# Down projections of two MLPs by Strassen's scheme, with the block sums on GpSimd

## What is computed

```
def _sqrelu_mlp(h, w1, w2):
    u = jax.nn.relu(h @ w1)
    return (u * u) @ w2
...
        h = h + _sqrelu_mlp(_rmsnorm(h, mlp_norm_g[i]), mlp_w1[i], mlp_w2[i])
```

## Time and profile before

| | us |
|---|---|
| median of 3 runs | 2151.53 |
| lowest and highest | 2151.14, 2152.66 |
| the profiled execution | 2150.84 |
| its span, first to last instruction | 2149.2 |
| PE busy in the span | 2111.7 |
| DVE, ACT, POOL busy | 1237.6, 847.6, 294.5 |

### The profile page before, as it was taken

How to read it: one execution, slowest core, us unless ns; L and a number is a source line. 1 busy time by engine, 2 the same in 40 slices (tenths; PEclk the granted TensorE clock), 3 DMA queues, 4 the chain that set the end, 5 groups by cost and what they waited for, 6 DMA issues and landing times.

```text
span 2149.2 us, 27349 instructions
## 1 busy us (share of the span) xinstructions
PE 2111.7 (98%) x9798; PEld 1749.3 (81%) x9798; DVE 1237.6 (58%) x1837; ACT 847.6 (39%) x1363; POOL 294.5 (14%) x330
## 2 busy tenths in 40 slices
PE   8999999999999999999999999999999999999998
PEld 6888888788888888777888888877888888888887
DVE  6464554663454553887645445557765456656674
ACT  4433343432222344776322222447662234433342
POOL 3223132300000011443100000302310010000001
PEclk9999999999999999999999999999999999999999
DMA  5232323233333232222233232321223322333332
GB/s 191 74 98 74 98 64 98 70 115 111 117 101 117 89 103 89 89 74 73 93 99 98 88 103 93 104 84 55 74 78 104 90 96 89 112 104 117 98 97 70
DMA packets 58530, 203.53 MB, mean 95 GB/s; under 512 B 6937, under 2 KB 9129, under 8 KB 58448
## 3 DMA queue, kind: packets, MB, share of 16 engines
q1 hardware_dynamic: 54304, 189.82, 28.1%
q0 software_dynamic: 3712, 11.95, 1.7%
q10 hardware_dynamic: 432, 0.66, 0.1%
HBM read 200.27 MB, written 6.06 MB: 96 GB/s over the span
## 4 chain that ended last, share of the span: by engine, by line
PE 90%; DVE 4%; ACT 4%; issue 1%; POOL 0%; DMA 0%; DVEq 0%; ACTq 0%; POOLq 0%
PE bank L520 29%; PE bank L521 28%; PE bank L522 28%; PE bank L755 1%; DVE w_lo L1535 1%; ACT arena L1245 1%; ACT arena_r L1264 1%; ACT w_hi L1055 1%; PE bank L770 1%; PE bank L768 1%; PE bank L734 0%; ACT arena_r L1258 0%; DVE arena L1789 0%; DVE h L1585 0%; POOL arena L2274 0%
## 5 line engine op out<-in xcount | busy, mean ns | idle before, releaser
L1535 DVE TENSOR_TENSOR w_lo<-raw,w_hi 128x1024 fp32r<-128x1024 f32 x354 | 462.4, 1308 | 272.4 <-ACT w_hi L1055 272.1
L520 PE MATMUL bank<-x_hi,w_hi 128*128 128x512 f32 x1552 | 613.7, 395 | 1.4 <-issue 0.7
L522 PE MATMUL bank<-x_hi,w_lo 128*128 128x512 f32 x1552 | 604.5, 390 | 0.0
L521 PE MATMUL bank<-x_lo,w_hi 128*128 128x512 f32 x1552 | 604.1, 389 | 0.0
L1055 ACT ACTIVATE w_hi<-raw 128x1024 fp32r<-128x1024 f32 x354 | 371.2, 1052 | 386.2 <-PE bank L522 385.1
L520 PE MATMUL bank<-arena_r,w_hi 128*128 128x512 f32 (+1 forms) x1040 | 400.1, 385 | 6.0 <-DVE h L1585 2.7
L522 PE MATMUL bank<-arena_r,w_lo 128*128 128x512 f32 (+1 forms) x1040 | 398.0, 383 | 0.0
L521 PE MATMUL bank<-arena_r,w_hi 128*128 128x512 f32 (+1 forms) x1040 | 397.9, 383 | 0.0
L520 PEld LDWEIGHTS bank<-x_hi,w_hi 128*128 128x128 f32 x1552 | 291.5, 188 | 64.2 <-issue 4.2
L521 PEld LDWEIGHTS bank<-x_lo,w_hi 128*128 128x128 f32 x1552 | 291.6, 188 | 61.7 <-issue 3.1
L522 PEld LDWEIGHTS bank<-x_hi,w_lo 128*128 128x128 f32 x1552 | 291.3, 188 | 61.3
(11 more groups left out here) (230 smaller groups left out, 1989.4 us busy)
## 6 DMA issues: line engine op xcount, KB each, us to landing
raw<-in_stream SPq DMA_DIRECT2D x354, 512.0 KB, 3.5
arena<-in_rel_pad POOLq DMA_DIRECT2D x16, 256.0 KB, 3.2
bias_strips<-bias_strip_once POOLq DMA_DIRECT2D x12, 320.0 KB, 4.2
out_t<-h SPq DMA_DIRECT2D x8, 256.0 KB, 2.2
h<-in_x_t SPq DMA_DIRECT2D x6, 256.0 KB, 8.4
arena<-in_c_decay POOLq DMA_DIRECT2D x4, 256.0 KB, 2.9
arena<-bias_strips POOLq DMA_DIRECT2D x4, 256.0 KB, 4.3
arena<-bias_strips POOLq DMA_DIRECT2D x8, 128.0 KB, 2.4
```

Of the source, the lines that this page charges most:

```text
L520: pe.matmul(dst, lh, rh, start=start, stop=False, **kw)
L521: pe.matmul(dst, lh, rl, start=False, stop=False, **kw)
L522: return pe.matmul(dst, ll, rh, start=False, stop=stop, **kw)
L1535: dve.tensor_tensor(w_lo[:, s, :], raw[:, s, :], f32(w_hi[:, s, :]), ALU.subtract).then_inc(lo_ready, 1)
```

## The change

A down stage multiplies the 1024 x 1024 block of w2 by a 1024 x 512 activation matrix. It is now cut into pairs: the positions into two halves of 256 (`QUARTER`), the hidden tiles into even and odd ones, the output tiles into pairs n = 0 to 3. For each pair of output tiles that is a 2 x 2 by 2 x 2 block product, A (weights) times B (activations), made with seven products in place of eight:

- weight blocks of 128 x 512: A11, A12, A21, A22 are the four halves of two units (the hidden tiles are reordered on the host so that a unit's halves are the even and the odd ones); S1 = A21 + A22, S2 = S1 - A11, S3 = A11 - A21, S4 = A12 - S2;
- activation blocks of 128 x 256 for each of four k: B11, B21, B22, and T1 to T4, sums of these.

The eight sums are made by GpSimd in fp32 (`combos`, `block_sums`). Each block is then rounded by ACT (`combo_his`, `block_his`) and its low part made by DVE (`combo_los`, `block_los`), for seven activation blocks and seven weight blocks. `w_hi` and `w_lo` hold eight block slots now. A product is 4 k-steps of three matmuls of 256 columns. Products with the same place in the output accumulate in banks 4 to 7; after each one or two products DVE adds the bank to a half of a tile of h (`add`, L1943), 31 additions a stage, counted in `quarter_read`, and PE waits for that count before it goes on in the bank. The arithmetic saves products that are partial sums of others by adding a bank more than once.

The core of the diff:

```diff
-                    proj(us, first=[(u_lo, Lin(base, 8, i))])
-                    for _ in range(7):
-                        proj(us)
+                    down_seven(Lin(g, 1, i))
                     for _ in range(8):
                         proj()
...
+            def product(slot, b, bank, fresh, ready, read=None, combos=None):
+                (wh, wl), (of, count) = block_at(slot), ready
+                wait(pe, of, count)
+                if read is not None:
+                    wait(pe, quarter_read, read)
+                for kk in range(4):
+                    if combos is not None:
+                        wait(pe, combo_lo, combos + 5 * kk)
+                    a = kk * P
+                    m = mm3(banks[bank][:, 0:QUARTER], (wh[:, a:a + P], wl[:, a:a + P]), tuple(combo(kk, b)),
+                            fresh and kk == 0, kk == 3, False)
+                m.then_inc(products_done, 1)
+                at.pe = at.pe + 1
+
+            def down_seven(g):
+                u, made, rd = at.u, g * 20, g * 31
+                product(0, B11, 4, True, (block_lo, made + nth_a11(0)), combos=made + 1)
+                product(2, T1, 6, True, (block_lo, made + nth_s1(0)), combos=made + 2)
+                product(3, B21, 7, True, (block_lo, made + nth_a12(0)), combos=made + 3)
+                product(5, T2, 4, False, (block_lo, made + nth_s2(0)), rd + 1, combos=made + 4)
+                product(6, B22, 6, False, (lo_ready, u + 1), rd + 2)
+                for n in range(1, 4):
+                    x, x_old, seen = 4 + n % 2, 5 - n % 2, rd + (7 * n - 2)
+                    product(0, B11, x, True, (block_lo, made + nth_a11(n)), seen - 2 if n > 1 else None)
+                    if n == 1:
+                        wait(pe, combo_lo, made + 20)
+                    product(1, T3, x_old, False, (block_lo, made + nth_s3(n - 1)), seen - 1)
+                    product(2, T1, 6, True, (block_lo, made + nth_s1(n)), seen)
+                    product(3, B21, 7, True, (block_lo, made + nth_a12(n)))
+                    product(4, T4, x_old, False, (lo_ready, u + 2 * n), seen + 2)
+                    product(5, T2, x, False, (block_lo, made + nth_s2(n)))
+                    product(6, B22, 6, False, (lo_ready, u + (2 * n + 1)), seen + 3)
+                product(7, T3, 4, True, (block_lo, made + nth_s3(3)), rd + 24)
+                product(4, T4, 7, True, (lo_ready, u + 8))
...
+                def add(bank, j, half, done, behind=None):
+                    wait(dve, products_done, p + done)
+                    if behind is not None:
+                        wait(dve, quarter_read, rd + behind)
+                    part = h[:, j, half * QUARTER:(half + 1) * QUARTER]
+                    dve.tensor_tensor(part, banks[bank][:, 0:QUARTER], part, ALU.add).then_inc(quarter_read, 1)
...
+            def combos(g, kk):
...
+                pool.tensor_tensor(t1, even[:, QUARTER:S], even[:, 0:QUARTER], ALU.subtract).then_inc(combo_sum, 1)
...
+                pool.tensor_tensor(t2, odd[:, QUARTER:S], t1, ALU.subtract).then_inc(combo_sum, 1)
...
+                pool.tensor_tensor(t3, odd[:, QUARTER:S], even[:, QUARTER:S], ALU.subtract).then_inc(combo_sum, 1)
...
+                pool.tensor_tensor(t4, odd[:, 0:QUARTER], t2, ALU.subtract).then_inc(combo_sum, 1)
...
+            def block_sums(g, n, u):
...
+                pool.tensor_tensor(s1f, weights(u, 1, 0), weights(u, 1, 1), ALU.add).then_inc(block_sum, 1)
...
+                pool.tensor_tensor(s2f, s1f, weights(u, 0, 0), ALU.subtract).then_inc(block_sum, 1)
+                pool.tensor_tensor(weights(u, 1, 0), weights(u, 0, 0), weights(u, 1, 0), ALU.subtract)\
+                    .then_inc(block_sum, 1)
...
+                pool.tensor_tensor(s4f, weights(u, 0, 1), s2f, ALU.subtract).then_inc(block_sum, 1)
```

297 lines of the change are left out of this document (249 added, 48 removed).

## The result

The changed kernel takes **2199.42 us** (median of 4 runs, 2197.32 to 2200.59) against 2151.9 for the kernel before in the same comparison. The ratio is 1.022, 95% interval 1.0202 to 1.0237: slower by 2.2%. The profiled execution took 2199.88 us; its span is 2198.2, which is 49.0 more than the 2149.2 of the earlier trace rows.

What follows compares the result with a forecast made beforehand. PE was taken to bound the kernel by matmul count times spacing, plus its waits. 6 x 1.0 + 2 x 11 + 4 + 5 = 37 us on the profiled 2150.84 gave 2188 us, range 2150 to 2206.

Steps and rivals of the forecast that it cites:

- products alone, a stage: PE in a down stage: 336 matmuls of 256 columns at 0.120 us, 40.32 us in place of 43.52.
- start of a stage, three waits: PE waits for DVE's additions before the fourth, fifth and seventh product of a down stage: 1.6, 0.2 and 2.3 us.
- six ordinary stages: Down stages other than each MLP's last: 44.5 us each, +1.0 us for each of six, bounds 41.0 and 47.5.
- two last stages: Last down stage of each MLP, also carrying the next stage's inputs: ends at 54.5 us, +11 us each.
- tails: Work after each MLP's last product delays the next projection: +4 us, and +5 after the second MLP; bounds 0 and 8 each.
- PE idle, "in all": Sign for the changed kernel: PE idle 25 to 70 us in all, where it was said to be small before.
- the exclusion: DVE operations with two SBUF inputs and GpSimd tensor operations exclude each other; DVE needs 0.55 us more (512 wide) after GpSimd.
- ACT's order: Last down stages: x_hi and square ahead of high halves on ACT make DVE stand 2.0 us three times, 1.3 twice.
- Rival 1: Faster, 2128 us: GpSimd sums fall beside DVE's additions and idle time, addition 4 ready before 10.4 us; chance 0.12.
- Rival 3: Slower, above 2206 us: PE's instruction stream makes the first four products 1.8 us each, eight stages add 12 us; chance 0.06.
- so three pairs hold: Later column pairs of a down stage: DVE 10.4 us against PE's 10.08, covered by 2.2 us of slack in additions.
- that is hidden: Raw weights in a down stage: a unit lands 3.5 us after its slot is free, its S1 sum wanted some 2 later.

Runs made afterwards that it cites:

- sums thin: The changed kernel with every GpSimd sum done on its first 16 columns only, all waits and signals kept: 2151.89 us, ratio 1.000.
- sums in the kernel before: The kernel before, with 96 unread 512-column GpSimd sums added in the first MLP: 2151.45 us, ratio 0.9998.
- the same edits of order: On the changed kernel: DVE additions earlier, GpSimd sums held back, strips in up stages; last stages in old form 2145.08 us, scheme throughout (ACT reordered too) 2168.8 us.

## Why the prediction came out as it did

The sign and the range were right (2188 forecast, 2150 to 2206, 2199.4 measured), the size was 11 us short: 7.5 in the ordinary stages, 3.7 in the last ones. The ordinary stages alone lie above the +12 that the range's high end gave them; the range held because the other terms stayed below theirs, which is some luck. By its own steps:

| step | forecast | measured |
|---|---|---|
| products alone, a stage | 40.32 | 40.5, sums thin |
| start of a stage, three waits | 1.6 + 0.2 + 2.3 | 1.3 + 0.25 + 2.1 |
| low halves, 512 wide | near 1.0 | 1.04 and 0.98 |
| six ordinary stages | +6 | +13.5 |
| two last stages | +11 and +11 | +9.5 and +16.2 |
| tails | +4 and +5 | +4.2 and +4.7 |
| up stages | 0 | 0 |
| PE idle, "in all" | 25 to 70 | 47.3 in the down stages, 88.3 in all |

The sign on PE's idle time was badly put: the kernel before had 37.5 us of it already, so only the share of the down stages fits the range. These eight stages together take 387.3 us, 64.7 more than 8 x 40.32.

**Right, and shown.** The pace of 256 columns; the exclusion as the cause of the waits at the start (thin sums, DVE's timeline without a gap, sums in the kernel before), and the hand-worked queue on DVE: additions 1, 2 and 4 were put at 5.7, 7.4 and 12.5 us and came at 5.5, 7.2 and 12.2. A stage with these waits alone is 44.17 where 44.4 to 44.5 was forecast. ACT's order is 13 of the 26 us of the last stages, with the clock in it. Rival 1 fell at the point it named; its 41 us come true only without the sums. Rival 3 fell: with the sums thin, PE's own stream costs 0.2 us a stage.

**Failed: "so three pairs hold" and "that is hidden".** Of the ordinary stages' +13.5, the known waits make 6 x 0.65 = 3.9. Another 6.7 is the third pair in the first MLP, with one half-clock stretch behind the longest of its waits. In the second MLP, without strips, three pairs do hold: a stage of 44.17 has no wait but those of its start. I had costed a weight's landing at the 3.5 us of the earlier trace rows, its median over the kernel, and had not followed what else the change moved: the strips, which GpSimd issued one by one all over the MLP, and now issues three to a stage right where two units are asked for. The prediction named no cost for them. The run with the strips moved gave 5.5 us of the three stages back, that stretch with them.

**Not in the sum: the clock.** The remaining 2.9 is two half-clock stretches at 1.4 us. Of the others one is the stretch just named, two lie in the second MLP's last stage, two in the tails and one in the attention layer, where one head takes 7.0 instead of 5.5 us. A term for it could not come from the trace of before, which has no wait in an MLP; PE waits of 2.1 us were forecast, what the clock does with them was not.

**Mis-sized: the second last stage.** I gave both last stages 11 us; the first took 9.5, the second 16.2. There ACT makes an extra square and GpSimd an extra sum for each tile, which I counted in the tail only. POOL is busy 36.7 us in that stage, 30.9 in the other. Two half-clock stretches, some 3 us, are also in it. At 59.7 us it lies outside the 50 to 56 given as a sign. No run takes the extra square and sum out, so their share is argued; with the block sums thin this stage was still 5.3 us longer than the other, 1.4 of it a half-clock stretch.

## What to carry to other kernels

Before work is put on an idle GpSimd, ask which DVE instructions it will meet: those with two SBUF inputs and the sums take turns (here a low half with its addition went from 0.93 to 1.70 us), and it matters only where DVE has a queue that the bound engine waits for. Where a scheme trades work of the bound engine for work of two others, split it by stage and keep it only in the stages whose helpers have room: here, with the same edits of order, six stages of eight gained 0.3% and all eight lost 0.8%; as changed, all eight lost 2.2%. When code moves on an engine, follow its DMA starts too, since what they collide with is not the engine.

## What was not expected of the hardware

- A wait of PE of 2 us can cost 1.4 us more than itself (3.41 us with 256-column matmuls 0.213 apart in place of 0.120), some 1.7 with 512 columns, since TensorE's granted clock is at 0.50 for 3.41 us behind it: at 14 of 30 waits of 2.1 us, one of three of 2.8, six of six of 3.9 and 5.1.
- A load of 512 KB that lands in 3.5 us with one other load behind it took 5.0 and 5.3 us with a 320 KB copy in flight as well, at up to 279 GB/s moved; in the first stage it took 6.7 with the copy and 5.1 without.
- GpSimd's sum of 512 columns takes 1.05 us where both inputs are the same columns (median of the 96 sums in the kernel before) and 1.29 where they differ.
